# LayerNorm's end as two three-input VectorE operations per token tile, without GpSimd's bias addition, and the weight split moved behind them

## The chip, the cores and the metric

The kernel runs on one core of a Trainium2 chip. The metric is the device time of one execution in microseconds, smaller is better. Names used below: PE is TensorE (PEld its weight loads), DVE is VectorE, ACT is ScalarE, POOL is GpSimd, SP is the engine whose queue issues the weight loads.

## The reference, cut to what matters

Two post-norm layers over 256 tokens of width 1024. Each of the four sub-layers ends in the same LayerNorm, and the next sub-layer starts from its result:

```python
def layer_norm(x, g, b):
    xf = x.astype(F32)
    mu = jnp.mean(xf, axis=-1, keepdims=True)
    var = jnp.mean(jnp.square(xf - mu), axis=-1, keepdims=True)
    return ((xf - mu) * lax.rsqrt(var + LN_EPS)).astype(x.dtype) * g + b

for layer in range(DEPTH):                      # DEPTH = 2
    if layer % 2 == 0:
        h = even_mixer(x, ...)                  # HGRN2 + dilated attention, output projection
        x = layer_norm(DEEPNORM_ALPHA * x + h, ev_ln1_g[j], ev_ln1_b[j])
        h = swiglu(x, ev_w1[j], ev_w3[j], ev_w2[j])
        x = layer_norm(DEEPNORM_ALPHA * x + h, ev_ln2_g[j], ev_ln2_b[j])
    else:
        h = odd_mixer(x, ...)                   # differential attention, output projection
        x = layer_norm(DEEPNORM_ALPHA * x + h, od_ln1_g[j], od_ln1_b[j])
        h = moe_swiglu(x, od_router[j], ...)    # top 2 of 8 experts
        x = layer_norm(DEEPNORM_ALPHA * x + h, od_ln2_g[j], od_ln2_b[j])
```

## The kernel before, in words

The 256 tokens are two tiles of 128 partitions, t = 0 and t = 1. `x[:, t, :]` holds a tile's 1024 float32 values. Everything is issued by hand: each engine has one program in a fixed order, and semaphores are the only link between engines. `link(ins)` makes DVE (or POOL) wait for its own instruction before it starts the next one.

Matrix products are made exact enough by splitting both sides into a high and a low part. SP loads a weight tile into `raw`, ACT rounds it to `whi` (`split_hi`, L279), DVE subtracts to get `wlo` (`split_lo`, L286), and PE multiplies three times (L305 to L307, or L1271 to L1273 in `last_group`). SP may refill a `raw` tile once its `wlo` is made. A group is four such tiles, j = 0 to 3; those read behind stage 1 are 1024 wide, those behind stages 0 and 2 1408 wide.

The end of a sub-layer is `end_of_stage`. PE's `last_group` gives the rows of t = 0 first and those of t = 1 some 5 us later. For each tile DVE adds the residual (L826), takes statistics (L827) and joins them to mean and variance in `mv` (L830). POOL then turns the variance into the reciprocal root `ln_rs` with two one-column operations (L451, L452). DVE normalizes (L836) and multiplies by the gain (L837). The bias is added by POOL for t = 0 (L457) and by DVE for t = 1 (L842). For t = 1, DVE splits tile j = 0 of the next group between the statistics and the normalization, while POOL makes the root.

Behind it PE transposes each finished tile of `x` (L1256, eight 128x128 blocks: waits `ln_done0` or `ln_done1`), ACT copies each bank to `xT_hi` (L555), DVE makes `xT_lo` (L820), and the next group's products begin when the third bank's `xT_lo` is there. This happens three times in that form or nearly so: `ev_ln1` before the SwiGLU (called stage 0 here, i = 0), `ev_ln2` before the odd input projection (stage 1), `od_ln1` before the router (stage 2). In stage 2 the transposed `x` goes to `xT_f` (ACT L735, DVE L1098), and the router's products (L1565) of t = 0 stand on PE between the transposes of the two tiles. The fourth, `od_ln2` (stage 3), ends the kernel: both tiles are normalized in a row, POOL makes both roots ahead of its bias addition, and SP sends each tile to `out` (L430).

Between stage 2 and stage 3 the eight experts run; that is more than half of the time.

Of the kernel before, what the change touches and what calls it, by code (L numbers as in the profile page):

```python
# [15 lines left out]
ALU = mybir.AluOpType  # L16
# [9 lines left out]
NT = S // P  # L26
# [81 lines left out]
def trunk(nc, a, c, out):  # L108

    with ExitStack() as ctx:  # L110
        sem = lambda name: ctx.enter_context(nc.semaphore(name))
# [6 lines left out]
        def at(name, shape, dt=F32, offset=None):  # L118
            size = int(np.prod(shape[1:])) * (1 if dt == U8 else 4)
            here = cur[0] if offset is None else offset  # L120
            if offset is None:
                cur[0] = here + (size + 31) // 32 * 32
            assert here + size <= top, (name, here + size, top)
            return nc.alloc_sbuf_tensor_at(name, shape, dt, offset=here), here + (size + 31) // 32 * 32

        def own(name, shape, dt=F32):
            return at(name, shape, dt)[0]
# [4 lines left out]
        x = own("x", [P, NT, D])  # L132
# [7 lines left out]
        mv = own("mv", [P, NT, 2])  # L140
        ln_rs = own("ln_rs", [P, NT])
# [7 lines left out]
        gains, after_gains = at("gains", [P, 2, D], F32, phase)  # L149
# [77 lines left out]
        t_ps, t_hi, t_lo = sem("t_ps"), sem("t_hi"), sem("t_lo")  # L227
        in_act, in_dve = sem("in_act"), sem("in_dve")
        ln_mv, ln_rstd = sem("ln_mv"), sem("ln_rstd")
        ln_gain, ln_done0, ln_done1, mix_done = sem("ln_gain"), sem("ln_done0"), sem("ln_done1"), sem("mix_done")  # L230
        up_silu, up_h = sem("up_silu"), sem("up_h")
        ht_ps, ht_hi, ht_lo = sem("ht_ps"), sem("ht_hi"), sem("ht_lo")
        g_sig, g_k, g_f, g_ln, g_hi, g_lo, g_lev = (sem(n) for n in ("g_sig", "g_k", "g_f", "g_ln", "g_hi", "g_lo", "g_lev"))
# [47 lines left out]
        def split_lo(dve, q, par, shapes, js=range(GT), in_late=False):  # L281
            for j in js:
                kc, n = shapes[j]
                dve.wait_ge(hi_done, 2 * GT * q + GT * par + j + 1)
                src = late[j] if in_late else raw[GT * par + j]
                nc.vector.tensor_tensor(wlo[j][:, 0:kc * n], src[:, 0:kc * n],  # L286
                                        whi[j][:, 0:kc * n].bitcast(F32), ALU.subtract).then_inc(lo_done, 1)
# [5 lines left out]
        def group_used(q, par):  # L293
            return 2 * GT * q + GT * (par + 1)
# [31 lines left out]
        def dn_src(w2, half, part):  # L326
            return [w2[:, k0:k0 + kc, half * NB:(half + 1) * NB] for k0, (kc, _) in zip(DN_K0[part], G_DN[part])]
# [9 lines left out]
        def dn_src_e(e, half, part):  # L337
            return [m_w2[:, bass.ds(e, 1), k0:k0 + kc, half * NB:(half + 1) * NB].rearrange("p e k n -> p (e k) n")
                    for k0, (kc, _) in zip(DN_K0[part], G_DN[part])]

        TURNS = [(0, 4, 6, 3), (4, 4, 7, 4), (8, 4, 6, 5), (12, 4, 7, 6), (16, 3, 6, 7), (19, 3, 3, None)]
        TURN_AFTER = {after: g for g, (_, _, _, after) in enumerate(TURNS) if after is not None}
        GATHER_AFTER = 2

# [88 lines left out]
        def _(pool):  # L435
# [14 lines left out]
            def rsqrt(dst, src, scale):  # L450
                link(nc.gpsimd.tensor_scalar(dst, src, scale, EPS, ALU.mult, ALU.add))  # L451
                return nc.gpsimd.tensor_tensor(dst, dst, neg_half[:, 0:dst.shape[1]], ALU.pow)  # L452

            def add_bias(i):

                pool.wait_ge(ln_gain, i + 1)
                nc.gpsimd.tensor_tensor(x[:, 0, :], x[:, 0, :], gains[:, 1, :], ALU.add).then_inc(ln_done0, 1)  # L457

            def ln_rsqrt(i):
                for t in range(NT):  # L460
                    pool.wait_ge(ln_mv, NT * i + t + 1)
                    rsqrt(ln_rs[:, t:t + 1], mv[:, t, 1:2], 1.0).then_inc(ln_rstd, 1)
                    if t == 0 and i < 3:
                        add_bias(i)
                if i == 3:
                    add_bias(i)

            def rotate(src, t, tmp, done):

# [26 lines left out]
            for t in range(NT):  # L496
                link(nc.gpsimd.tensor_tensor(proj[:, t, GA:GA + 512], proj[:, t, GA:GA + 512],
                                             sga[:, t, :], ALU.mult))
                v = proj[:, t, GA:GA + 512].rearrange("p (h c) -> p h c", h=AH)
# [18 lines left out]
            rms_heads(0, on0, proj[:, :, GA:GA + 512].rearrange("p t (h c) -> p t h c", h=4), proj[:, :, 0:512])  # L518
            load_gains(0, "ev_ln1_g", "ev_ln1_b")
            ln_rsqrt(0)  # L520
            load_gains(1, "ev_ln2_g", "ev_ln2_b")
            ln_rsqrt(1)


# [14 lines left out]
            for t in range(NT):  # L539
                pool.wait_ge(r_ms, 3 + t)  # L540
                rsqrt(vec[:, 40 + 4 * t:44 + 4 * t], vec[:, 32 + 4 * t:36 + 4 * t], 1.0 / AD).then_inc(r_rs, 1)
            ln_rsqrt(2)
            pool.wait_ge(ln_done1, 3)
            nc.gpsimd.memset(ones[:], 1.0).then_inc(ones_set, 1)
# [264 lines left out]
        def _(dve):  # L809
            n_link = [0]  # L810

            def link(ins):
                n_link[0] += 1
                ins.then_inc(dve_link, 1)
                dve.wait_ge(dve_link, n_link[0])
# [7 lines left out]
            def residual(bank, half, t):  # L823

                v = x[:, t, half * NB:(half + 1) * NB]
                link(nc.vector.scalar_tensor_tensor(v, v, ALPHA, psum[:, bank + t, :], ALU.mult, ALU.add))  # L826
                link(nc.vector.bn_stats(stat[:, t, half, :], v))  # L827

            def mean_var(t):
                nc.vector.bn_aggr(mv[:, t, :], stat[:, t, :, :].rearrange("p a b -> p (a b)")).then_inc(ln_mv, 1)  # L830

            def normalize(i, t):
                v = x[:, t, :]
                dve.wait_ge(gain_in, 32 * (i + 1))
                dve.wait_ge(ln_rstd, NT * i + t + 1)
                link(nc.vector.tensor_scalar(v, v, mv[:, t, 0:1], ln_rs[:, t:t + 1], ALU.subtract, ALU.mult))  # L836
                ins = nc.vector.tensor_tensor(v, v, gains[:, 0, :], ALU.mult)  # L837
                if t == 0:
                    ins.then_inc(ln_gain, 1)
                else:  # L840
                    link(ins)
                    nc.vector.tensor_tensor(v, v, gains[:, 1, :], ALU.add).then_inc(ln_done1, 1)  # L842

            def end_of_stage(i, q, bank, nxt):

                for t in range(NT):
                    if t == 0:
                        dve.wait_ge(rows_done, i + 1)
                    else:
                        dve.wait_ge(tile_used, group_used(q, 1))  # L850
                    residual(bank, 1, t)
                    mean_var(t)
                    if t == NT - 1:
                        split_lo(dve, *nxt, js=(0,))
                    normalize(i, t)

            def sum_squares(r, sq):
                dve.wait_ge(r_sq, r + 1)
                nc.vector.tensor_reduce(vec[:, 32:40].rearrange("p (t h) -> p t h", h=4), sq, AX_X, ALU.add).then_inc(r_ms, 1)
# [117 lines left out]
            for t in range(NT):  # L977
                ins = nc.vector.tensor_tensor(proj[:, t, 512:1024].rearrange("p (h c) -> p h c", h=BH),
                                              psum[:, 6 + t, :].rearrange("p (h c) -> p h c", h=BH),
                                              rinv[:, t, :, None].broadcast_to([P, BH, BD]), ALU.mult)  # L980
# [3 lines left out]
            def out_projection(i, q, nxt):  # L984
                split_lo(dve, q, 1, G_SQ)
                dve.wait_ge(tile_used, group_used(q, 0))
                for t in range(NT):
                    residual(0, 0, t)
                end_of_stage(i, q, 2, nxt)
# [32 lines left out]
            for t in range(NT):  # L1022
                residual(4, 0, t)
            split_lo(dve, Q_DN + 1, 1, G_DN[1])
            end_of_stage(1, Q_DN + 1, 6, (Q_IN2, 0, G_SQ))
            transposed_lo(3)
            split_lo(dve, Q_IN2, 0, G_SQ, js=(1, 2, 3))
# [213 lines left out]
            for t in range(NT):  # L1241
                normalize(3, t)
# [452 lines left out]
```

## Time and profile before

| what | value |
|---|---|
| median of 3 runs | 1432.72 us (1431.81 to 1433.81) |
| profiled execution, span from first to last instruction | 1432.0 us |
| PE busy | 1340.4 us (94%) |
| DVE busy | 1095.1 us (76%) |
| ACT busy | 841.0 us (59%) |
| POOL busy | 117.3 us (8%) |
| mean granted clock of PE | 0.957 |

The profiled execution's time is not listed apart from its span; the span lies inside the range of the three runs and 0.7 us below their median. Starts below are counted from the beginning of the span. The granted clock is a share of full speed: 1.00 is 2.4 GHz and 0.50 is 1.2 GHz. A row of the timeline reads: start, duration, engine, line, operation, output<-inputs, shape, and in brackets how long the engine sat idle before it and what ended that.

### The profile page before, as it was taken

Reading aid. Unit: us, or ns where it says so; the run is one execution under the profiler, and the core shown is the slowest. Engines: PE = TensorE matmul, PEld = TensorE weight load, DVE = VectorE, ACT = ScalarE, POOL = GpSimd, SP = SyncE. Lnnn points to the kernel's source line nnn. Section 1 sums busy time; section 2 is a strip of 40 time slices with the busy share of each in tenths; the row PEclk is TensorE's granted clock in tenths of the full one; section 3 lists DMA queues with packets and bytes.
Section 4 is the critical chain, followed back from the end, with each engine's and each line's share of the span. In section 5 each row is a group of like instructions: output and inputs, shape, how many; then the busy total and the mean of one; then the engine's idle time right before and its main releaser. Section 6 shows DMA issues by size and latency. Waiting matters only on the chain.

```text
span 1432.0 us, 20794 instructions
## 1 busy us (share of the span) xinstructions
PE 1340.4 (94%) x7430; PEld 1221.9 (85%) x7430; DVE 1095.1 (76%) x1056; ACT 841.0 (59%) x884; POOL 117.3 (8%) x91
## 2 busy tenths in 40 slices
PE   6997898999898976799999999999999999999995
PEld 5887787999686865699899899898998998998994
DVE  4777646444455995669889889989989888898987
ACT  3555333433333463267768767768667677687772
POOL 1044201000001922100000000000000000000001
PEclk9998878999998997799999999999999999999998
DMA  9552025665345531769999999999999999999980
GB/s 331 184 191 68 1 87 175 183 198 188 118 118 178 166 125 25 240 237 329 344 331 347 358 327 346 364 321 342 360 330 346 365 326 347 330 346 355 370 305 31
DMA packets 227056, 359.02 MB, mean 251 GB/s; under 512 B 8400, under 2 KB 155984, under 8 KB 226880
## 3 DMA queue, kind: packets, MB, share of 16 engines
q1 hardware_dynamic: 225344, 351.50, 71.9%
q0 software_dynamic: 1664, 6.88, 1.4%
q8 instruction: 30, 0.49, 0.2%
q14 instruction: 18, 0.15, 0.0%
HBM read 357.30 MB, written 1.05 MB: 250 GB/s over the span
## 4 chain that ended last, share of the span: by engine, by line
PE 86%; DVE 9%; issue 2%; ACT 1%; POOL 1%; DMA 1%; SPq 0%; DVEq 0%; ACTq 0%
PE psum L305 25%; PE psum L307 24%; PE psum L306 24%; DVE wlo L286 3%; PE psum L1583 2%; PE psum L1597 1%; PE psum L1423 1%; DMA raw<-in_ev_w_in 1%; DVE x L837 1%; PE psum L1256 1%; PE psum L1359 1%; PE psum L1339 1%; PE psum L1407 1%; PE psum L1273 1%; PE psum L1399 1%
## 5 line engine op out<-in xcount | busy, mean ns | idle before, releaser
L286 DVE TENSOR_TENSOR wlo<-raw,whi 128x1408 fp32r<-128x1408 f32 (+2 forms) x500 | 794.6, 1608 | 229.4 <-ACT whi L279 224.6
L279 ACT CAST whi<-raw 128x1408 fp32r<-128x1408 f32 (+2 forms) x500 | 661.6, 1328 | 343.5 <-PE psum L307 312.8
L305 PE MATMUL psum<-whi,xe_hi 128*128 128x352 f32 x1024 | 332.4, 325 | 1.3 <-DVE mv L1215 1.3
L307 PE MATMUL psum<-whi,xe_lo 128*128 128x352 f32 x1024 | 330.6, 323 | 0.0
L306 PE MATMUL psum<-wlo,xe_hi 128*128 128x352 f32 x1024 | 330.4, 323 | 0.0
L305 PEld LDWEIGHTS psum<-whi,xe_hi 128*128 128x128 f32 x1024 | 192.4, 188 | 2.0 <-issue 1.4
L305 PE MATMUL psum<-whi,xT_hi 128*128 128x352 f32 (+1 forms) x512 | 186.3, 364 | 8.3 <-DVE wlo L286 6.1
L306 PEld LDWEIGHTS psum<-wlo,xe_hi 128*128 128x128 f32 x1024 | 192.4, 188 | 0.6
L307 PEld LDWEIGHTS psum<-whi,xe_lo 128*128 128x128 f32 x1024 | 192.4, 188 | 0.0
L306 PE MATMUL psum<-wlo,xT_hi 128*128 128x352 f32 (+1 forms) x512 | 185.2, 362 | 0.0
L307 PE MATMUL psum<-whi,xT_lo 128*128 128x352 f32 (+1 forms) x512 | 184.7, 361 | 0.0
L305 PE MATMUL psum<-whi,hTe_hi 128*128 128x512 f32 x352 | 140.6, 399 | 0.0
L306 PE MATMUL psum<-wlo,hTe_hi 128*128 128x512 f32 x352 | 139.3, 396 | 0.0
L307 PE MATMUL psum<-whi,hTe_lo 128*128 128x512 f32 x352 | 139.2, 395 | 0.0
L305 PEld LDWEIGHTS psum<-whi,xT_hi 128*128 128x128 f32 x512 | 98.2, 192 | 20.7 <-issue 6.7
L307 PEld LDWEIGHTS psum<-whi,xT_lo 128*128 128x128 f32 x512 | 98.3, 192 | 10.6
L306 PEld LDWEIGHTS psum<-wlo,xT_hi 128*128 128x128 f32 x512 | 98.3, 192 | 10.1
L451 POOL TENSOR_SCALAR ln_rs<-mv 128x1 f32<-128x1 f32 x8 | 4.9, 612 | 1086.4 <-DVE mv L830 1086.1
L307 PEld LDWEIGHTS psum<-whi,hTe_lo 128*128 128x128 f32 x352 | 66.2, 188 | 15.9
L306 PEld LDWEIGHTS psum<-wlo,hTe_hi 128*128 128x128 f32 x352 | 66.2, 188 | 15.3
L305 PEld LDWEIGHTS psum<-whi,hTe_hi 128*128 128x128 f32 x352 | 66.2, 188 | 15.2
L762 ACT ACTIVATE silu_e<-psum 128x352 f32<-128x352 f32 x64 | 29.7, 464 | 37.6 <-PE psum L307 37.6
(244 smaller groups left out, 1305.3 us busy)
## 6 DMA issues: line engine op xcount, KB each, us to landing
raw<-in_od_w SPq DMA_DIRECT2D x256, 704.0 KB, 6.1
raw<-in_od_w SPq DMA_DIRECT2D x94, 768.0 KB, 6.2
raw<-in_ev_w SPq DMA_DIRECT2D x32, 704.0 KB, 4.2
raw<-in_ev_w_in SPq DMA_DIRECT2D x32, 512.0 KB, 5.4
raw<-in_od_w SPq DMA_DIRECT2D x30, 512.0 KB, 6.1
raw<-in_od_w_in SPq DMA_DIRECT2D x24, 512.0 KB, 3.8
raw<-in_ev_w SPq DMA_DIRECT2D x12, 768.0 KB, 4.5
raw<-in_ev_w_out SPq DMA_DIRECT2D x8, 512.0 KB, 4.4
```

The source lines that it names most:

```text
L279: nc.scalar.copy(whi[j][:, 0:kc * n], src[:, 0:kc * n]).then_inc(hi_done, 1)
L286: nc.vector.tensor_tensor(wlo[j][:, 0:kc * n], src[:, 0:kc * n], whi[j][:, 0:kc * n].bitcast(F32), ALU.subtract).then_inc(lo_done, 1)
L305: nc.tensor.matmul(ps, hi[:, k, t0:t0 + P], w_h, start=(k == first_k), stop=False)
L306: nc.tensor.matmul(ps, hi[:, k, t0:t0 + P], w_l, start=False, stop=False)
L307: last = nc.tensor.matmul(ps, lo[:, k, t0:t0 + P], w_h, start=False, stop=(k == last_k))
L762: nc.scalar.activation(silu_e[:, b % 2, :], psum[:, 2 * (b % 2), 0:NU], ACT.Silu).then_inc(m_silu, 1)
L837: ins = nc.vector.tensor_tensor(v, v, gains[:, 0, :], ALU.mult)
L1256: ins = nc.tensor.transpose(psum[:, 4 + 2 * t + kb, kk * P:(kk + 1) * P], src(4 * kb + kk, t), ident)
L1273: ins = nc.tensor.matmul(ps, lo[:, k, t * P:(t + 1) * P], w_h, start=False, stop=(k == last_k))
L1339: nc.tensor.matmul(dst, lf_hi[:, t, d, h * AD:(h + 1) * AD], m, start=True, stop=False)
L1359: ins = nc.tensor.matmul(dst, k_[:, ts * P:(ts + 1) * P], q_[:, tt * P:(tt + 1) * P], start=True, stop=True)
L1583: ins = nc.tensor.matmul(psum[:, 4 + k // 4, (k % 4) * P:(k % 4 + 1) * P], xn[:, t, k * P:(k + 1) * P], pick[:, t, :], start=(t == 0), sto ...
```

## The change

`normalize` is now two `scalar_tensor_tensor` operations on DVE for both tiles: (x - mean) * gain, which needs only the mean, and then (that) * root + bias, which needs POOL's root. `add_bias` on POOL and its semaphore `ln_gain` are gone. In `end_of_stage` the split of tile j = 0 of the next group stands behind both normalizations instead of before that of t = 1.

```diff
-            def add_bias(i):
-
-                pool.wait_ge(ln_gain, i + 1)
-                nc.gpsimd.tensor_tensor(x[:, 0, :], x[:, 0, :], gains[:, 1, :], ALU.add).then_inc(ln_done0, 1)
-
             def ln_rsqrt(i):
                 for t in range(NT):
                     pool.wait_ge(ln_mv, NT * i + t + 1)
                     rsqrt(ln_rs[:, t:t + 1], mv[:, t, 1:2], 1.0).then_inc(ln_rstd, 1)
-                    if t == 0 and i < 3:
-                        add_bias(i)
-                if i == 3:
-                    add_bias(i)
...
             def normalize(i, t):
                 v = x[:, t, :]
                 dve.wait_ge(gain_in, 32 * (i + 1))
+                dve.wait_ge(ln_mv, NT * i + t + 1)
+                link(nc.vector.scalar_tensor_tensor(v, v, mv[:, t, 0:1], gains[:, 0, :], ALU.subtract, ALU.mult))
                 dve.wait_ge(ln_rstd, NT * i + t + 1)
-                link(nc.vector.tensor_scalar(v, v, mv[:, t, 0:1], ln_rs[:, t:t + 1], ALU.subtract, ALU.mult))
-                ins = nc.vector.tensor_tensor(v, v, gains[:, 0, :], ALU.mult)
-                if t == 0:
-                    ins.then_inc(ln_gain, 1)
-                else:
-                    link(ins)
-                    nc.vector.tensor_tensor(v, v, gains[:, 1, :], ALU.add).then_inc(ln_done1, 1)
+                nc.vector.scalar_tensor_tensor(v, v, ln_rs[:, t:t + 1], gains[:, 1, :], ALU.mult,
+                                               ALU.add).then_inc(ln_done1 if t else ln_done0, 1)
...
                     residual(bank, 1, t)
                     mean_var(t)
-                    if t == NT - 1:
-                        split_lo(dve, *nxt, js=(0,))
                     normalize(i, t)
+                split_lo(dve, *nxt, js=(0,))
```

What stands on DVE at the end of stage 0, before, from the statistics of t = 0 to the low parts of the transposed tile (BN_AGGR is the joining of the statistics):

```order
126 L830 BN_AGGR mv<-stat 128x2
127 L836 TENSOR_SCALAR x<-x,mv,ln_rs 128x1024
128 L837 TENSOR_TENSOR x<-x,gains 128x1024
129 L826 SCALAR_TENSOR_TENSOR x<-x,psum 128x512
130 L827 BN_STATS stat<-x 128x6
131 L830 BN_AGGR mv<-stat 128x2
132 L286 TENSOR_TENSOR wlo_61<-raw_49,whi_57 128x1408
133 L836 TENSOR_SCALAR x<-x,mv,ln_rs 128x1024
134 L837 TENSOR_TENSOR x<-x,gains 128x1024
135 L842 TENSOR_TENSOR x<-x,gains 128x1024
136 L820 TENSOR_TENSOR xT_lo<-psum,xT_hi 128x4x128 x4
```

The same place of the change (its lines are numbered anew: L817, L818, L821 and L811 are the old L826, L827, L830 and L820):

```order
126 L821 BN_AGGR mv<-stat 128x2
127 L827 SCALAR_TENSOR_TENSOR x<-x,mv,gains 128x1024
128 L829 SCALAR_TENSOR_TENSOR x<-x,ln_rs,gains 128x1024
129 L817 SCALAR_TENSOR_TENSOR x<-x,psum 128x512
130 L818 BN_STATS stat<-x 128x6
131 L821 BN_AGGR mv<-stat 128x2
132 L827 SCALAR_TENSOR_TENSOR x<-x,mv,gains 128x1024
133 L829 SCALAR_TENSOR_TENSOR x<-x,ln_rs,gains 128x1024
134 L286 TENSOR_TENSOR wlo_61<-raw_49,whi_57 128x1408
135 L811 TENSOR_TENSOR xT_lo<-psum,xT_hi 128x4x128 x4
```

The split of `wlo_61` moved from ahead of the normalization of t = 1 to behind it, and three passes over the tile of t = 1 became two.

POOL's program from the gains of stage 0 to those of stage 1, before (DMA rows are loads of gain and bias):

```order
39 L447 DMA gains<-in_ev_ln_g 128x1024
40 L448 DMA gains<-in_ev_ln_b 128x1024
41 L451 TENSOR_SCALAR ln_rs<-mv 128x1
42 L452 TENSOR_TENSOR ln_rs<-ln_rs,neg_half 128x1
43 L457 TENSOR_TENSOR x<-x,gains 128x1024
44 L451 TENSOR_SCALAR ln_rs<-mv 128x1
45 L452 TENSOR_TENSOR ln_rs<-ln_rs,neg_half 128x1
46 L447 DMA gains<-in_ev_ln_g 128x1024
```

And with the change:

```order
39 L447 DMA gains<-in_ev_ln_g 128x1024
40 L448 DMA gains<-in_ev_ln_b 128x1024
41 L451 TENSOR_SCALAR ln_rs<-mv 128x1
42 L452 TENSOR_TENSOR ln_rs<-ln_rs,neg_half 128x1
43 L451 TENSOR_SCALAR ln_rs<-mv 128x1
44 L452 TENSOR_TENSOR ln_rs<-ln_rs,neg_half 128x1
45 L447 DMA gains<-in_ev_ln_g 128x1024
```

Only the two pairs that make the roots are left there; the bias addition between them is gone.

## Rows read from the trace of the kernel before

**Rows 1.** The page: busy time of each engine and its share of the span.

```profile
PE 1340.4 (94%) x7430; PEld 1221.9 (85%) x7430; DVE 1095.1 (76%) x1056; ACT 841.0 (59%) x884; POOL 117.3 (8%) x91
```

**Rows 2.** Waits, 640 to 1400 us: total us, times, longest us.

```profile
ACT whi L279 <- PE psum L307: 145.7, 210, 2.0
```

**Rows 3.** Timeline of DVE, end of stage 0.

```profile
222.69 0.69 DVE L826 SCALAR_TENSOR_TENSOR x<-x,psum 128x512 f32<-128x512 f32 x1 [0.59 <-PE psum L1273]
...
224.14 0.21 DVE L830 BATCH_NORM_AGGREGATE mv<-stat 128x2 f32<-128x12 f32 x1
224.27 1.75 DVE L286 TENSOR_TENSOR wlo<-raw,whi 128x1408 fp32r<-128x1408 f32 x1
226.80 0.81 DVE L836 TENSOR_SCALAR x<-x,mv,ln_rs 128x1024 f32<-128x1024 f32 x1 [0.79 <-POOL ln_rs L452]
...
228.91 1.23 DVE L842 TENSOR_TENSOR x<-x,gains 128x1024 f32<-128x1024 f32 x1
230.05 1.28 DVE L820 TENSOR_TENSOR xT_lo<-psum,xT_hi 128x512 fp32r<-128x512 f32 x2
...
240.60 1.63 DVE L286 TENSOR_TENSOR wlo<-raw,whi 128x1408 fp32r<-128x1408 f32 x1 [2.49 <-ACT whi L279]
```

**Rows 4.** Timeline of POOL, end of stage 0.

```profile
219.07 0.19 POOL L451 TENSOR_SCALAR ln_rs<-mv 128x1 f32<-128x1 f32 x1 [40.02 <-DVE mv L830]
...
222.18 2.36 POOL L457 TENSOR_TENSOR x<-x,gains 128x1024 f32<-128x1024 f32 x1 [2.26 <-DVE x L837]
224.62 1.45 POOL L451 TENSOR_SCALAR ln_rs<-mv 128x1 f32<-128x1 f32 x1
226.15 0.54 POOL L452 TENSOR_TENSOR ln_rs<-ln_rs,neg_half 128x1 f32<-128x1 f32 x1
```

**Rows 5.** Timelines of PE and ACT, end of stage 0.

```profile
224.59 1.09 PE L1256 MATMUL psum<-small,x 128*128 128x128 f32 x8 [1.94 <-POOL x L457]
230.19 1.97 PE L1256 MATMUL psum<-small,x 128*128 128x128 f32 x8 [4.50 <-DVE x L842]
232.71 0.66 PE L305 MATMUL psum<-whi,xT_hi 128*128 128x352 f32 x1 [0.55 <-DVE xT_lo L820]
...
231.34 0.59 ACT L555 CAST xT_hi<-psum 128x512 fp32r<-128x512 f32 x1 [4.98 <-PE psum L1256]
```

**Rows 6.** Timelines of DVE and PE, end of stage 1.

```profile
433.30 0.21 DVE L830 BATCH_NORM_AGGREGATE mv<-stat 128x2 f32<-128x12 f32 x1
...
441.29 0.80 PE L305 MATMUL psum<-whi,xT_hi 128*128 128x512 f32 x1 [0.55 <-DVE xT_lo L820]
```

**Rows 7.** Timelines of DVE, ACT and PE, end of stage 2.

```profile
586.05 0.21 DVE L830 BATCH_NORM_AGGREGATE mv<-stat 128x2 f32<-128x12 f32 x1
...
594.10 0.69 DVE L1098 COPY xT_f<-psum 128x512 f32<-128x512 f32 x1 [2.06 <-PE psum L1256]
...
580.58 5.45 ACT L279 CAST whi<-raw 128x1408 fp32r<-128x1408 f32 x4 [5.75 <-PE psum L1273]
587.24 1.07 ACT L735 COPY xT_f<-psum 128x512 f32<-128x512 f32 x2 [1.22 <-PE psum L1256]
...
588.36 2.78 PE L1565 MATMUL psum<-router,xT_f 128*128 128x8 f32 x16 [0.73 <-ACT xT_f L735]
592.09 1.97 PE L1256 MATMUL psum<-small,x 128*128 128x128 f32 x8 [0.95 <-DVE x L842]
```

**Rows 8.** Timeline of DVE, end of stage 3, the kernel's last operations.

```profile
1420.35 0.28 DVE L830 BATCH_NORM_AGGREGATE mv<-stat 128x2 f32<-128x12 f32 x2
...
1424.44 3.24 DVE L837 TENSOR_TENSOR x<-x,gains 128x1024 f32<-128x1024 f32 x1
1427.72 1.23 DVE L842 TENSOR_TENSOR x<-x,gains 128x1024 f32<-128x1024 f32 x1
```

**Rows 9.** One line's instructions: ns min/median/max, first and last start.

```profile
L1070 DVE SCALAR_TENSOR_TENSOR aP<-eP,vec x16: 483/484/487, 520.0 to 548.8; 128x256 f32<-128x256 f32 x16
```

**Rows 10.** One stretch: us, busy by engine, granted clock, DMA share, GB/s.

```profile
232.70:237.40 4.70, 4.69 (x16) 4.69 (x17) 4.59 (x4) 0.08 (x1) 0.00 (x0) 0.50 0.75 217
```

More of the change, by code:

```diff
@@ L229, in trunk @@
         ln_mv, ln_rstd = sem("ln_mv"), sem("ln_rstd")
-        ln_gain, ln_done0, ln_done1, mix_done = sem("ln_gain"), sem("ln_done0"), sem("ln_done1"), sem("mix_done")
+        ln_done0, ln_done1, mix_done = sem("ln_done0"), sem("ln_done1"), sem("mix_done")
         up_silu, up_h = sem("up_silu"), sem("up_h")
```

## The prediction, made before the run

> **What bounds the kernel now.** I read the page first: PE is busy for 1340.4 us, 94% of the span [rows 1], so a gain must come out of PE's some 90 idle us. Then the waits by stretch. In the experts' part ACT waits for PE 210 times, 145.7 us in total [rows 2]: PE sets the pace, and whatever arrives earlier at its start passes through to the end. Then the timelines at the ends of the four stages, where the LayerNorm is what PE waits for. In stage 0 PE idles 1.94 us until POOL's bias addition of t = 0 and 4.50 us until DVE's of t = 1, then transposes and waits 0.55 us more for `xT_lo` [rows 5]. Only t = 1 counts: its residual (222.69) itself waits for PE's last product [rows 3], so t = 0 can end anywhere before some 222.6 us without moving it, and the transposes of t = 0 (1.09 us [rows 5]) fit into the wait for t = 1.
>
> **The price of the new operation.** No row shows a three-input operation with 1024 elements and both tensors in SBUF. The nearest is L1070: same operation, same kinds of operands (per-partition scalar, two float32 tensors in SBUF), 256 elements, 0.484 us [rows 9]. Two-input passes over 1024 and 512 elements take 1.23 and 0.69 us, 1.05 ns an element [rows 3, 7]. So 0.484 + 768 x 0.00105 = 1.29 us. A lower bound is the 1.23 us of L842; the upper is below, under the rivals.
>
> **When the root comes.** This decides where the second operation starts. In stage 0, t = 0, the statistics end 0.09 us before POOL's first root operation at 219.07, that takes 0.19 us [rows 4]. But for t = 1 the same one-column operation took 1.45 us: it began at 224.62 and ended at 226.07, just after DVE's split of `wlo` (224.27 to 226.02), and `wlo` needed 1.75 us instead of 1.63 where POOL's bias addition was still running at its start [rows 3, 4]. So a DVE pass with two SBUF tensors and a POOL operation shut each other out. The new first operation is such a pass and starts some 0.04 us behind the statistics, ahead of POOL. I take it that POOL waits for its end: 0.05 to finish the first, 0.09 to the second, 0.54 for it [rows 4], 0.11 until DVE goes on (the root was there at 226.69, L836 began at 226.80 [rows 3, 4]): 0.79, taken as 0.80 us. The Trainium skill says of two-input `tensor_tensor` what these rows show ("SBUF — State Buffer", section "Who interferes with whom": a VectorE instruction with two SBUF inputs contends with a GpSimd instruction that reads SBUF); applied to the three-input form it gives the same 0.80. With no shutting out the root would come 0.9 us after the statistics, hidden under the first operation, and the second would follow at once: bounds of 0.04 and 0.80 us.
>
> **Stage 0.** Statistics of t = 1 end at 224.35 [rows 3]. First operation 224.39 to 225.68, second from S = 226.48 to 227.77; before, the bias ended at 230.14 [rows 3]. That is 2.37 us earlier for the transposes. But the split of tile j = 0, which lay in the wait for the root, now lies behind: 1.63 us [rows 3], overlapping its neighbour by 0.09 us as rows 3 show for L842 and L820. DVE then makes `xT_lo`, one each 0.59 us (two in 1.28, one in 0.69 [rows 3, 7]). The third begins at S + 1.20 + 1.53 + 2 x 0.59 = S + 3.91 and ends at S + 4.60. ACT's copy for it would be done earlier: 1.15 us from the transposes' start to the copy, 0.59 for it [rows 5], so S + 1.35 + 1.74 = S + 3.09. DVE sets the end, so some 0.8 us of the gain goes back to the moved split. PE starts at S + 4.66 = 231.14 instead of 232.71 [rows 5]: **-1.57 us**. POOL's 2.36 us [rows 4] were never on that path, except that they let the transposes of t = 0 wait.
>
> **Stage 1.** Same sum: statistics end 433.51 [rows 6], S = 433.51 + 0.04 + 1.29 + 0.80 = 435.64, the split is one of 1024 elements (1.23 us as L842), PE at S + 4.27 = 439.91 instead of 441.29 [rows 6]: **-1.38 us**.
>
> **Stage 2.** Here t = 0 counts too, since its router products stand on PE ahead of the transposes of t = 1. Before, they began at 588.36 behind copies that waited for POOL's bias addition [rows 7]. Now the transposes of t = 0 follow PE's last product at 584.6 and are done by 585.7, ACT is free at 586.03, copies in 1.07 us, and the products run from 587.06 to 589.84. The tile t = 1 is ready at 586.26 + 0.04 + 1.29 + 0.80 + 1.29 = 589.68. So the transposes start at 589.86 instead of 592.09 [rows 7], and the split of j = 0 (to 591.2) lies under their 1.97 us; then L1098 and all of the routing follow as before: **-2.23 us**.
>
> **Stage 3.** Both statistics precede. First operation of t = 0 from 1420.6 to 1421.9, its second from 1422.7 to 1424.0, the first of t = 1 right behind to 1425.2. POOL's second root finds no gap and comes after that: 0.80, so the last operation runs from 1426.0 to 1427.3. Before, the end was 1428.95, of which 2 us stand in one L837 of 3.24 us where L842 takes 1.23: it waited for POOL's bias addition [rows 8]. Sending out t = 1 follows as before: **-1.7 us**, and up to 2.4 if a root slips in between two DVE operations.
>
> Nothing is added elsewhere: the split of j = 0 lets SP refill one `raw` tile some 3 us later in stage 0, while in the 10 us behind ACT waits for PE, not for loads. The removed bias additions also free POOL for the next gains.
>
> **Sum.** 1.57 + 1.38 + 2.23 + 1.7 = 6.9 us. The profiled span is 1432.0 us, 0.7 below the median of 1432.72; against the runs I forecast 1432.7 - 6.9 = **1425.8 us** (0.48% less).
>
> **PE's clock.** After the wait in stage 0 PE ran at 0.50, the lower level (1.2 GHz): from 232.7 to 237.4 us the granted clock was 0.50 [rows 10]. The remaining wait (some 4 us instead of 4.5) will not spare that. If full speed returned at the same moments as before, the 1.57 and 1.38 us would be spent at half speed and be worth half: 1.5 us less gain. If it comes as long after the restart as before, nothing is lost. I take the latter; a stretch that ends somewhat sooner or later adds about 1 us of scatter either way.
>
> **Rivals.**
> 1. *POOL isn't shut out by the three-input pass.* For: rows 3 and 4 show it for two-input passes only. Then S is 0.76 us earlier in stages 0 and 1 (-2.33, -2.14), stage 2 stays with its router products (-2.2), and stage 3 runs four operations in a row, 1420.6 + 4 x 1.29 = 1425.8 (-3.2): -9.9, 1422.8 us. Chance 0.20.
> 2. *Three-input passes at half rate, the slower side.* The price of 1.29 rests on L1070. If 1024 elements took twice the streaming time, 2.35 us (of 1.29 the 1.07 that 1024 elements take at 1.05 ns are doubled), t = 0 in stage 0 would end at 224.6 and push the residual of t = 1 back by 1.8 us. Working the stages through: +2.5, +1.0, +1.6, +2.5, so +7.6, 1440.3 us; the whole turns into a loss from 1.8 us an operation on. Against: 0.484 us for 256 elements leaves no room for it, it would be 0.75 [rows 9]. The Trainium skill speaks for this rival: "Vector Engine (DVE) Microarchitecture Reference", section "Points that are easy to get wrong", has it that this form with two SBUF sources that aren't bf16 halves throughput; by that rule it would be 1440, by the row 1425.8. I follow the row. Chance 0.04.
> 3. *The gain sinks in PE's restart.* The earlier starts run at half speed and the low-clock stretches, those of the routing in stage 2 too, come out longer: half of stages 0 and 1 lost (1.5 us) and another 1 us in each of the three restarts leave 2.4 us, 1430.3 us, within 0.2%. Against: it takes all three together. Chance 0.08.
>
> The forecast itself has 0.68. About 0.2% (2.9 us) is what a measurement of this kernel tells from no change.
>
> **How the numbers follow.** The forecast's own range is 1424.3 (roots slipping in) to 1427.5 (half speed). The range takes in rival 1 with its scatter and leaves rivals 2 and 3 out: 1422.0 to 1428.5. Faster by over 0.2%: forecast and rival 1, 0.88; within: rival 3, 0.08; slower: rival 2, 0.04.
>
> **What the changed profile would show.** Three-input passes of 1.29 us, eight of them (2.35 would be rival 2). POOL's first root operation at t = 1 some 1.3 us long, ending with the first pass, and a gap of 0.8 us on DVE before the second (no gap: rival 1). PE's wait for t = 1 in stage 0 down to about 4.1 us, but its wait for `xT_lo` up to some 1.3 us. The 3.24 us operation gone. Wrong would be a residual of t = 1 that starts later than 0.1 us behind PE's last product, or expert parts that are longer than before.

## The result, and the profile after

The changed kernel took 1426.26 us (median of 5 runs, 1421.45 to 1426.92), the one before 1433.43 us beside it (5 runs, 1431.81 to 1433.81 but for one of 2193.13 us, which was disturbed and is left out of the comparison). The ratio is 0.9948 with a 95% interval of 0.9931 to 0.9966. Run again later (`e9_after_again`), the changed kernel took 1421.64 us (6 runs) against 1431.39 us (11 runs), ratio 0.9939 (0.9918 to 0.9959). The forecast was 1425.8 us, a ratio of 0.9952. It holds in sign and size. That the first comparison meets it within 0.5 us is partly luck: the four stages gained 8.7 us, not the 6.9 forecast, and in that profile the stretches between them gave 1.7 us back (see "Where those 1.7 us went" below).

I read the four stages one by one, in numbers that don't depend on where a stage begins: from the end of the joined statistics of t = 1 to the first product behind it (stages 0 and 1), to the start of the last bank's copy on DVE (stage 2), and to the end of the last pass (stage 3).

| stage | before, us | changed, us | difference | forecast |
|---|---|---|---|---|
| 0 | 8.36 | 6.56 | -1.80 | -1.57 |
| 1 | 7.78 | 6.16 | -1.62 | -1.38 |
| 2 | 7.84 | 5.25 | -2.59 | -2.23 |
| 3 | 8.32 | 5.64 | -2.68 | -1.7 |
| sum | 32.30 | 23.61 | -8.69 | -6.9 |

Page of the changed kernel, span and busy time. PE is as busy as in [rows 1]; 7.0 us of span are gone, DVE has 4 us less to do and POOL 7:

```profile
span 1425.0 us, 20794 instructions
...
PE 1341.2 (94%) x7430; PEld 1223.8 (86%) x7430; DVE 1091.1 (77%) x1052; ACT 840.6 (59%) x884; POOL 110.5 (8%) x87
```

One line's instructions in the changed kernel (ns: min, median, max): the first of the two new passes.

```profile
L827 DVE SCALAR_TENSOR_TENSOR x<-x,mv,gains x8: 1276/1285/1287, 218.6 to 1419.4; 128x1024 f32<-128x1024 f32 x8
```

Timelines of DVE, POOL and PE at the end of stage 0 in the changed kernel, for t = 1; they answer to [rows 3], [rows 4] and [rows 5]:

```profile
223.67 0.21 DVE L821 BATCH_NORM_AGGREGATE mv<-stat 128x2 f32<-128x12 f32 x1
223.98 1.28 DVE L827 SCALAR_TENSOR_TENSOR x<-x,mv,gains 128x1024 f32<-128x1024 f32 x1
225.77 1.28 DVE L829 SCALAR_TENSOR_TENSOR x<-x,ln_rs,gains 128x1024 f32<-128x1024 f32 x1 [0.51 <-POOL ln_rs L452]
226.97 1.62 DVE L286 TENSOR_TENSOR wlo<-raw,whi 128x1408 fp32r<-128x1408 f32 x1
228.51 2.48 DVE L811 TENSOR_TENSOR xT_lo<-psum,xT_hi 128x512 fp32r<-128x512 f32 x4
...
223.96 0.19 POOL L451 TENSOR_SCALAR ln_rs<-mv 128x1 f32<-128x1 f32 x1 [3.63 <-DVE mv L821]
224.24 1.43 POOL L452 TENSOR_TENSOR ln_rs<-ln_rs,neg_half 128x1 f32<-128x1 f32 x1
...
222.02 1.03 PE L1243 MATMUL psum<-small,x 128*128 128x128 f32 x8
227.11 1.97 PE L1243 MATMUL psum<-small,x 128*128 128x128 f32 x8 [4.06 <-DVE x L829]
230.44 0.66 PE L305 MATMUL psum<-whi,xT_hi 128*128 128x352 f32 x1 [1.36 <-DVE xT_lo L811]
```

The reader is to see four things. The pass takes 1.28 us. POOL's second root operation takes 1.43 us instead of 0.54 and ends at 225.67, 0.41 us after the first pass (225.26): it was held up while the pass ran (`e3` and `e4` below test this). PE's wait for the tile is down from 4.50 to 4.06 us, and its wait for `xT_lo` up from 0.55 to 1.36: that is the moved split. The first of these waits shrinks so little because the transposes of t = 0 end earlier too; counted from the joined statistics of t = 1, the tile is ready after 3.17 us instead of 5.79. And between the split and the four `xT_lo` DVE has no gap, so DVE sets the start of the products.

The end of the kernel, DVE and POOL, answering to [rows 8]. The operation of 3.24 us is gone. POOL's second L452 (18.46 to 19.90) ends while the first pass of t = 1 is still running (to 20.69), so the last pass follows without a gap:

```profile
1416.08 0.28 DVE L821 BATCH_NORM_AGGREGATE mv<-stat 128x2 f32<-128x12 f32 x2
1416.39 1.28 DVE L827 SCALAR_TENSOR_TENSOR x<-x,mv,gains 128x1024 f32<-128x1024 f32 x1
1418.21 1.28 DVE L829 SCALAR_TENSOR_TENSOR x<-x,ln_rs,gains 128x1024 f32<-128x1024 f32 x1 [0.53 <-POOL ln_rs L452]
1419.41 1.28 DVE L827 SCALAR_TENSOR_TENSOR x<-x,mv,gains 128x1024 f32<-128x1024 f32 x1
1420.72 1.28 DVE L829 SCALAR_TENSOR_TENSOR x<-x,ln_rs,gains 128x1024 f32<-128x1024 f32 x1
...
1416.65 1.45 POOL L452 TENSOR_TENSOR ln_rs<-ln_rs,neg_half 128x1 f32<-128x1 f32 x1
...
1418.46 1.44 POOL L452 TENSOR_TENSOR ln_rs<-ln_rs,neg_half 128x1 f32<-128x1 f32 x1
```

### The profile page after: what moved, and what is told of

Its sections match the earlier page's. It is cut to its first block, busy times and chain, and to the rows that moved or that the text cites. A ratio compares the mean times of both kernels' runs of the same rounds, so it can differ in the third digit from the quotient of the medians.

```text
span 1425.0 us, 20794 instructions
## 1 busy us (share of the span) xinstructions
PE 1341.2 (94%) x7430; PEld 1223.8 (86%) x7430; DVE 1091.1 (77%) x1052; ACT 840.6 (59%) x884; POOL 110.5 (8%) x87
## 4 chain that ended last, share of the span: by engine, by line
PE 88%; DVE 8%; issue 2%; ACT 1%; DMA 1%; POOL 1%; SPq 0%; DVEq 0%; ACTq 0%
PE psum L305 25%; PE psum L307 25%; PE psum L306 25%; DVE wlo L286 3%; PE psum L1570 2%; PE psum L1584 1%; PE psum L1410 1%; DMA raw<-in_ev_w_in 1%; PE psum L1260 1%; PE psum L1258 1%; PE psum L1259 1%; PE psum L1346 1%; PE psum L1326 1%; PE psum L1394 1%; PE psum L1386 1%
## 5 line engine op out<-in xcount | busy, mean ns | idle before, releaser
L305 PEld LDWEIGHTS psum<-whi,xT_hi 128*128 128x128 f32 x512 | 98.7, 193 | 22.4 <-issue 6.8
L451 POOL TENSOR_SCALAR ln_rs<-mv 128x1 f32<-128x1 f32 x8 | 1.5, 190 | 1101.1 <-DVE mv L821 1101.0
```

Source lines behind the costliest of these rows:

```text
L305: nc.tensor.matmul(ps, hi[:, k, t0:t0 + P], w_h, start=(k == first_k), stop=False)
```

## The experiments

Before's median beside the first four runs was 1431.17 us (17 runs), beside the next three 1430.54 us (7 runs), beside the last two 1431.39 us (11 runs).

**Only the moved split** (`e1_move_only`). The kernel before, with this edit alone:

```diff
-                    if t == NT - 1:
-                        split_lo(dve, *nxt, js=(0,))
                     normalize(i, t)
+                split_lo(dve, *nxt, js=(0,))
```

> Only one part of the change: the three old passes and the bias addition on GpSimd stay, and the split of tile j = 0 moves behind the normalization of t = 1. I read each stage by itself, from the end of the joined statistics of t = 1 to the first product (stages 0 and 1), to the copy of the last bank (stage 2) and to the end of the last pass (stage 3): 8.36, 7.78, 7.84 and 8.32 us before, 32.3 in all; 6.56, 6.16, 5.25 and 5.64 us with the whole change, 23.6 in all. Theory A (the passes and their overlap with the root make the gain, the moved split gives part of it back): 7.8, 7.4, 6.9, 8.3, sum 30.4, so -1.9 us against before. Rival B (moving the split is what gains): a sum near 25. Totals scatter by some 2 us with the clock, the stage times do not.

Measured, stages 0 to 3: 7.93, 7.34, 6.58 and 8.31 us, sum 30.16; ratio 0.9989 (0.9975 to 1.0003), no difference that can be told. Theory A holds within 0.3 us in each stage. What the root no longer waits for is mostly paid back behind the normalization. Only stage 2, where the split disappears under the transposes, keeps 1.26 us.

**The change without the moved split** (`e2_split_back`), the same edit undone in the changed kernel:

```diff
+                    if t == NT - 1:
+                        split_lo(dve, *nxt, js=(0,))
                     normalize(i, t)
-                split_lo(dve, *nxt, js=(0,))
```

> The change without the moved split: the split of tile j = 0 stands before the normalization of t = 1 again. GpSimd's root now waits for the split instead of for the first pass. If it slips in between the split and the first pass (theory A, as seen in stage 3 of the change), the second pass starts at 2.87 us after the statistics in stage 0 and the stage times are 6.7, 6.3, 6.25 and 5.6 us, sum 24.9 (+1.3 against the change). If it has to wait for both (theory B), the second pass starts at 3.4 us and the sum is some 26.4.

Measured: 7.04, 6.65, 6.54 and 5.64 us, sum 25.87, between the two theories; ratio 0.9953 (0.9931 to 0.9974). DVE, then POOL, end of stage 0:

```profile
220.84 1.57 DVE L286 TENSOR_TENSOR wlo<-raw,whi 128x1408 fp32r<-128x1408 f32 x1
222.32 1.28 DVE L827 SCALAR_TENSOR_TENSOR x<-x,mv,gains 128x1024 f32<-128x1024 f32 x1
224.10 1.28 DVE L829 SCALAR_TENSOR_TENSOR x<-x,ln_rs,gains 128x1024 f32<-128x1024 f32 x1 [0.50 <-POOL ln_rs L452]
...
221.01 1.45 POOL L451 TENSOR_SCALAR ln_rs<-mv 128x1 f32<-128x1 f32 x1 [3.63 <-DVE mv L821]
222.54 1.46 POOL L452 TENSOR_TENSOR ln_rs<-ln_rs,neg_half 128x1 f32<-128x1 f32 x1
```

POOL's two operations were each held once: the first by the split (to 222.41; the operation ended at 222.46), the second by the pass (to 223.60; ended at 224.00). So the first did slip in at the boundary, as A said, but I had forgotten that the root is two operations and needs two gaps. Beside the changed kernel this order costs 2.3 us of stage time, 1.3 of them in stage 2: the moved split is worth that much together with the new passes, and 2.1 us on its own (`e1`). The new passes without the moved split gain 6.4 us (32.30 to 25.87), so the two parts of the change nearly add up to its 8.7 us.

**No overlap with the root** (`e3_root_first`):

```diff
                 dve.wait_ge(ln_mv, NT * i + t + 1)
+                dve.wait_ge(ln_rstd, NT * i + t + 1)
                 link(nc.vector.scalar_tensor_tensor(v, v, mv[:, t, 0:1], gains[:, 0, :], ALU.subtract, ALU.mult))
-                dve.wait_ge(ln_rstd, NT * i + t + 1)
```

> The change, but VectorE waits for the root before its first pass, so nothing overlaps the root and nothing shuts GpSimd out. Theory A (the change overlaps the root with the first pass, but the pass holds the root up until it ends, so only part of the root's 1.05 us is hidden): the root's second operation is 0.55 us long again instead of 1.45, the second pass starts 2.4 us after the statistics instead of 1.9, each stage +0.5 us, sum 25.6. If the overlap hid the whole root (rival), it would be +1.0 a stage, sum 27.5.

Measured: 7.03, 6.63, 5.71 and 6.12 us, sum 25.49 (25.6 by theory A); ratio 0.9941 (0.992 to 0.9961). L452 took 0.54 us again, and DVE waited 1.04 us for it. The overlap hides half of the root, 0.47 us a stage, 1.9 us in all. The other 6.8 us come from the fewer passes, the removed bias addition and the moved split together. In the totals this kernel can't be told from the change; the 1.9 us show in the stage times only.

**The first pass in two halves** (`e4_halves`):

```diff
-                link(nc.vector.scalar_tensor_tensor(v, v, mv[:, t, 0:1], gains[:, 0, :], ALU.subtract, ALU.mult))
+                a_, b_ = slice(0, NB), slice(NB, D)
+                nc.vector.scalar_tensor_tensor(v[:, a_], v[:, a_], mv[:, t, 0:1], gains[:, 0, a_], ALU.subtract, ALU.mult)
+                link(nc.vector.scalar_tensor_tensor(v[:, b_], v[:, b_], mv[:, t, 0:1], gains[:, 0, b_], ALU.subtract, ALU.mult))
```

> The change, with the first pass cut into two passes of 512 elements, back to back without a wait. Theory A (a pass with two SBUF tensors shuts GpSimd out until it ends, and GpSimd gets in between two passes): the root's second operation ends about 0.4 us after the first half, under the second half, and is some 0.9 us long instead of 1.45; the second full pass follows with a gap of 0.04 us at 1.55 us after the statistics instead of 1.9. Each stage -0.3 us, sum 22.4, although 0.2 us of VectorE time is added per tile. Rival (GpSimd waits until VectorE is idle): the root comes 0.5 us after the second half, the second pass starts at 2.1 us, sum 24.4.

Measured: 6.23, 5.82, 4.90 and 5.40 us, sum 22.35 (22.4 by theory A); ratio 0.9924 (0.9899 to 0.9949). DVE, then POOL, end of stage 0:

```profile
223.89 0.75 DVE L828 SCALAR_TENSOR_TENSOR x<-x,mv,gains 128x512 f32<-128x512 f32 x1
224.56 0.75 DVE L829 SCALAR_TENSOR_TENSOR x<-x,mv,gains 128x512 f32<-128x512 f32 x1
225.34 1.29 DVE L831 SCALAR_TENSOR_TENSOR x<-x,ln_rs,gains 128x1024 f32<-128x1024 f32 x1
...
224.15 0.90 POOL L452 TENSOR_TENSOR ln_rs<-ln_rs,neg_half 128x1 f32<-128x1 f32 x1
```

The root ends at 225.05, 0.41 us after the first half and under the second, so the last pass has no gap. Only the first pass was cut in two here, and the length of POOL's operation followed the length of the first piece (0.90 us beside 0.75 us, 1.43 beside 1.28): the holding up is shown, and so is that it ends with the instruction, not with DVE's work. `e2` to `e4` together decide against the prediction's rival 1.

**TensorE kept busy through the wait** (`e5_warm`). The changed kernel, with eight products nobody reads between the transposes of the two tiles in stages 0 and 1:

```diff
+                    if norm in (0, 1) and t == 0:
+                        keep_busy(0, 8)
+
+            def keep_busy(bank, count):
+                for _ in range(count):
+                    nc.tensor.matmul(psum[:, bank, 0:3 * P], ident, small[:].rearrange("p a b -> p (a b)"), start=True, stop=True)
```

> The change, plus eight products on TensorE whose results nobody reads (identity by 384 columns, into a bank that is free) between the transposes of the two tiles in stages 0 and 1, where TensorE idles 4.06 us. Theory C (the engine's idle wait is what lowers its clock to 0.50 for the transposes of t = 1 and the first 3 to 6 us of products behind them, so the wait costs more than its own length): the granted clock stays at 1.00 there, the eight transposes take 1.03 us instead of 1.97, and from the statistics of t = 1 in stage 0 to those in stage 1 it takes some 3 us less than the 207.97 us of the change; in all -5 us against the change, near 1420 us. Rival (the clock falls and rises whatever the engine does, or such products don't count as work): clock 0.50 as before, no gain, or a loss of up to 2 us where they run at half speed and delay the transposes.

Measured: 1419.32 us (4 runs), ratio 0.9924 (0.9908 to 0.9941). From the statistics of t = 1 in stage 0 to those in stage 1 it took 205.06 us instead of 207.97. The same stretch of time, 230 to 234 us, first in the changed kernel, whose first product starts at 230.44, then here, where it starts at 229.22 (us, busy by engine, granted clock, DMA share, GB/s):

```profile
230.00:234.00 4.00, 3.56 (x12) 3.56 (x13) 4.00 (x5) 0.00 (x0) 0.00 (x0) 0.50 0.99 343
```

```profile
230.00:234.00 4.00, 4.00 (x27) 4.00 (x26) 4.00 (x3) 0.58 (x1) 0.00 (x0) 1.00 0.96 327
```

The clock stays at 1.00 (2.4 GHz), the eight transposes take 1.04 us instead of 1.97, and a product follows the one before it by 0.16 us instead of 0.29. So theory C is shown for the clock. Its price is not: the unaltered change, profiled again in `e9`, took 205.46 us for the stretch that took 207.97 in its first profile, so by these profiles anything between 0.4 and 2.9 us may belong to the unread products. In the total, 1419.32 us is 4 us below the mean of the change's 11 runs (5 expected), but the intervals of the two ratios overlap (0.9918 to 0.9959 for `e9`). The stage times stay what they were (6.56, 6.17, 5.19, 5.65): the eight products take 5.33 us, run on for 1 us after the tile is ready and push the transposes back by as much as these got shorter, and DVE sets the start behind them.

**Less DVE work behind the last pass** (`e6_lean`). This goes on top of the halves. In stage 1 the split moves ahead of the residual, and in stages 0 and 1 (i = 2 and 3 in the first lines, which count other transposed tiles too) the low parts are made in the order in which PE needs them. The waits of PE, not shown, follow the new order:

```diff
-                for b in range(4):
+                for b in ((0, 2, 1, 3) if i in (2, 3) else range(4)):
                     dve.wait_ge(t_hi, 4 * i + b + 1)
...
                     else:
+                        if i == 1:
+                            split_lo(dve, *nxt, js=(0,))
                         dve.wait_ge(tile_used, group_used(q, 1))
...
-                split_lo(dve, *nxt, js=(0,))
+                if i != 1:
+                    split_lo(dve, *nxt, js=(0,))
```

> The change with the first pass in two halves, and VectorE's work behind the last pass made smaller: in stage 1 the split of tile j = 0 goes ahead of the residual of t = 1, where VectorE idles 2.1 us, and in stages 0 and 1 the low parts are made in the order of need (0, 2, 1, 3), so that the first product waits for two of them and not three. Theory (the moved split and the low parts set the start of the products, not the transposes and copies): stage 0 from 6.23 to 5.6, stage 1 from 5.82 to 5.4 (there the copy on ScalarE sets it then), the others as with the halves, sum 21.3 us. Rival (the transposes and the copy set it): no difference to the halves, 22.35.

Measured: 5.63, 5.41, 4.90 and 5.41 us, sum 21.35; ratio 0.9925 (0.9908 to 0.9941), the same as with the halves (0.9924); 4 or 5 runs don't show a difference of 1 us. The stage times are the forecast's to 0.05 us: DVE's queue set stages 0 and 1, not the copies.

**Both, and the routing too** (`e7_lean_warm`, `e8_lean_warm5`). `e6` with `keep_busy` in stages 0 and 1, in the router's waits (bank 1) and behind the router's and the positions' products (bank 3); `e8` has five products instead of eight in stages 0 and 1 and one fewer at two other places:

```diff
-                        keep_busy(0, 8)
+                        keep_busy(0, 5)
...
-                keep_busy(1, 2 if t else 4)
+                keep_busy(1, 2 if t else 3)
...
-            keep_busy(3, 3)
+            keep_busy(3, 2)
```

> The kernel of the previous run with products that keep TensorE busy in stages 0 and 1 and in the waits of the routing (behind the transposes of each tile, behind the router's products, behind the positions). Theory C: the clock stays at 1.00 from stage 2 to the experts, the gather of the first expert (32 products, 5.98 us at 0.50) takes about 3 us, the first copy in stage 2 comes 0.5 us earlier; some 9 us less than the lean kernel alone, near 1411 us. Rival: the additional products stand in the way of the short ones of the routing and give back what the clock brings, 1418 to 1420 us.

> The previous kernel with fewer of the products nobody reads: five instead of eight in stages 0 and 1 (eight took 5.33 us and ended 1 us after the tile was ready, so stage 0 and 1 came to 6.17 us each instead of 5.63 and 5.41), and one fewer at two places of the routing. Theory C: the clock stays at 1.00, the transposes of t = 1 start as soon as the last pass ends, stages 0 and 1 come down to about 5.6 and 4.9 us, 1.8 us less than before, near 1413.5 us. Rival: with fewer of them the engine idles long enough for its clock to fall again, and it lands between the lean kernel and this, near 1417 us.

Measured: `e7` 1415.53 us, ratio 0.9895 (0.9875 to 0.9914), 4 us above what I expected. The eight products held back the transposes of t = 1 for 1.3 us (tile ready at 224.25, transposes from 225.60), and stages 0 and 1 took 6.17 us each; by `e8` that explains 1.8 us, and the rest stays open. `e8` took 1409.15 us (5 runs), ratio **0.9863** (0.9842 to 0.9883), with stage times of 5.62, 4.95, 4.29 and 5.40 us, sum 20.26. It beats both kernels and was the fastest of all. The stage times are the forecast's, but the total is 4 us below it, and the stages don't explain that. PE of `e8` in stages 0 and 1, where the unread products (two records each) now end ahead of the tile, and the first expert's gather, 3.8 us instead of 5.98 before and 5.55 in `e6`:

```profile
219.80 3.39 PE L1255 MATMUL psum<-small 128*128 128x384 f32 x10
223.68 1.09 PE L1248 MATMUL psum<-small,x 128*128 128x128 f32 x8 [0.49 <-DVE x L831]
...
426.74 1.09 PE L1248 MATMUL psum<-small,x 128*128 128x128 f32 x8 [0.49 <-DVE x L831]
428.80 0.50 PE L305 MATMUL psum<-whi,xT_hi 128*128 128x512 f32 x1 [0.96 <-DVE xT_lo L811]
...
585.40 3.81 PE L1584 MATMUL psum<-pick,xn 128*128 128x128 f32 x32 [0.26 <-DVE gate_col L1125]
```

The profiled runs of `e6` and `e8` differ by 10.7 us, and not all of it is the unread products' work: 2.8 us lie ahead of the first of them. The four stages give 1.1 us and the stretch from stage 2 to stage 3, with the routing, 2.8 us; that stretch took 825.9 to 827.3 us in all nine profiles without unread products in the routing and 823.5 and 823.3 us in the two with them, so it is shown. The stretches from stage 0 to 1 (1.6 us) and 1 to 2 (2.4 us) differ by no more than they do between the two profiles of the change (2.5 and 3.3 us), so those 4 us are not shown.

**The change again** (`e9_after_again`), unchanged, for the interval.

> The change itself again, on the chip of the previous kernel, for a narrower interval. By stage times it should gain 8.7 us against before (32.30 less 23.61), a ratio of 0.9939; by the five runs seen so far 0.9948. If the stage times carry through in full, the mean of many runs lands near 0.994; if something gives 2 us of it back elsewhere, near 0.9955.

Measured: stage times 6.56, 6.16, 5.25 and 5.65 us, ratio 0.9939. Over all runs the mean is 1431.7 us before (39 runs, without the one of 2193 us) and 1423.4 us changed (11 runs): -8.3 us, close to the 8.69 of the stage times.

## Why the prediction was right, step by step

- **Only t = 1 counts in stages 0 and 1; PE's pace carries the gain through the experts.** Right. The residual of t = 1 still starts on PE's last product, and in the experts' part ACT waited for PE 144.7 us in 210 waits, as before [rows 2].
- **1.29 us a pass.** Right: 1.285 us. The row of 256 elements [rows 9] could be stretched to 1024. Rival 2 is refuted: half of the two-input rate would have been 2.35 us, and 512 elements took 0.75 us with both tensors in SBUF (`e4`) against 0.69 with one in PSUM (the residual). The Trainium skill ("Vector Engine (DVE) Microarchitecture Reference", section "Points that are easy to get wrong") states that this form halves its throughput with two SBUF sources that aren't bf16; the traces don't agree with it for the form used here.
- **When the root comes.** Right in kind, too large in size: 0.80 us after the first pass was forecast, 0.51 measured (225.26 to 225.77). POOL's first operation began 0.02 us ahead of the pass and took its usual 0.19 us, so only the second was held, and of that one 0.41 us were left when the pass ended. The pass itself began 0.10 us behind the statistics and not 0.04. Together that is 0.24 us in each of stages 0 and 1, which is the whole of their miss. The sign that I had named, a first root operation of 1.3 us that ends with the pass, did not come; the one that was held was the second.
- **Rival 1**, that POOL isn't shut out, is refuted by the profile and `e2` to `e4`, not by the time: it gave a gain of 9.9 us, and the 9.75 us between the medians in `e9` lie nearer to that than to the forecast's 6.9.
- **The moved split.** Right: behind the last pass it is on the path in stages 0 and 1, as the 1.36 us wait for `xT_lo` shows (some 1.3 forecast), and under the transposes in stage 2. What I had not worked out is that the move gains all the same, 2.3 us together with the new passes (`e2`). Its later refill of a `raw` tile cost nothing in stage 0: PE was busy without a break from 230.44 to 240 us.
- **Stage 2.** 2.59 us instead of 2.23: the router's products of t = 0 took 1.95 us instead of 2.78 [rows 7], since they now run at a granted clock of 1.00 (0.66 over the 2.78 us before), and then not they but the tile of t = 1, which came 0.24 us sooner with the root, set the start at 588.28.
- **Stage 3**, the term that was mis-sized most: -1.7 forecast, -2.68 measured. I had named 2.4 us as the case in which a root slips in between two DVE operations, and chose the other. It slipped in, and the first root came sooner as above.
- **PE's clock.** Neither of my two cases fits. Full speed came back 5.0 us behind the restart of stage 0 before, 5.9 us in the changed kernel and 3.2 us in its second profile (`e9`). I took the scatter as about 1 us. The runs of the change spread from 1417.88 to 1427.52 us. Each run's mean granted clock goes with its time: 0.957 at 1426.92 us, 0.967 at 1417.88 us (correlation -0.93 over 11 runs, -0.78 over 35 runs of before). The first comparison's 7.2 us against 8.7 in the stage times lies within that.
- **Where those 1.7 us went.** In the profiled runs the start was 0.5 us sooner, the stretch from stage 0 to 1 0.6 us longer, from stage 1 to 2 2.1 us longer (144.97 us before [rows 6, 7], 147.03 changed, 143.7 in `e9`), and from stage 2 to 3 0.5 us shorter. The 2.1 us lie at the start of the output projection behind the odd attention, which the change doesn't touch: its first products, from 558.90 us, still ran at a granted clock of 0.50 in the changed kernel, and from 562.51 us at 1.00 before. The same 4.8 us of it, changed and then before, 12 products against 21:

```profile
559.00:563.80 4.80, 4.80 (x12) 3.74 (x13) 0.69 (x1) 0.00 (x0) 0.00 (x0) 0.50 0.01 3
```

```profile
562.60:567.40 4.80, 4.80 (x21) 3.96 (x22) 1.40 (x2) 1.05 (x1) 0.00 (x0) 1.00 0.02 3
```

- **Rival 3** did not come: the stretch from stage 0 to 1 took 201.41 us in the changed kernel and 198.89 in `e9`, against 200.80 before, and the gain of 8.3 us over all runs is far from its 2.4.

## What to carry to other kernels

When a short GpSimd operation feeds VectorE, look at what VectorE does meanwhile: a long instruction that reads two SBUF tensors held GpSimd up until it ended in every case here (0.54 us became 1.43), so the overlap has to leave instruction boundaries, one for each GpSimd operation that meets such an instruction. Merging passes is worth their length only as far as no other work moves onto the path behind them; count the whole queue up to the engine that waits. And where TensorE idled for some 4 us, the products behind the wait ran at half speed for 3 to 6 us; a few unread products, kept shorter than the wait, avoided that. What it brings has to be measured on many runs, since the clock alone moves the total by as much.

## What the runs showed of the hardware that I had not expected

- GpSimd gets its turn between two VectorE instructions even where these follow without a gap (the second starts 0.08 us before the first ends): its one-column operation then ended 0.41 us after the boundary, under the next pass (`e4`, and stage 3 of the change).
- Five unread products of 384 columns in each of two waits, and thirteen in the routing, went with a granted clock of TensorE at 1.00 (in `e8` from 218 to 232, 424 to 434 and 571 to 591 us; in `e6` it was 0.64 from 578 to 602). By the ratios `e8` is 0.6% below `e6` (0.9925 to 0.9863); 3.9 us of that, 0.3%, are shown at the places of these products.
- The granted clock goes with differences of up to 10 us (0.7%) between runs of one and the same kernel, more than this change brings. Stage times from one profile told kernels apart that medians of five runs did not: those of the change and of its repetition agree within 0.01 us in each stage.
